# One core, a two-layer decoder trunk in split float32: the split weights stored 136 columns apart instead of 128

## The reference

```
for l in range(2):
    h = rmsnorm(x, norm1)
    z = h @ w_in                       # 1024 -> 6400 columns: attention, convolution, recurrence, gates
    ya, yb, yc = dilated_attention(z), gated_convolution(z), hgrn2_recurrence(z)
    mix = g0 * (ya @ w_pa) + g1 * (yb @ w_pb) + g2 * (yc @ w_pc)
    x = x + mix @ w_o
    h2 = rmsnorm(x, norm2)
    x = x + square(relu(h2 @ w_up)) @ w_down      # 1024 -> 4096 -> 1024
y = rmsnorm(x, norm_f)
```

## Time and profile before

| | |
|---|---|
| runs of the kernel | 811.49, 812.18 and 812.16 us, median 812.16 |
| profiled execution: span from first to last instruction | 809.8 us |
| profiled execution: its own time with what lies around the span | not shown; the median run is 2.4 us over the span |
| TensorE busy with matmuls, with weight loads | 99%, 98% of the span |
| VectorE, ScalarE, GpSimd busy | 70%, 54%, 34% |
| granted TensorE clock, mean of the span | 0.997 of full |
| matmul instructions | 6786 |
| HBM read, written | 191.17 MB, 51.90 MB |

### The profile page before, as it was taken

How to read it: one execution, slowest core, us unless ns; L and a number is a source line. 1 busy time by engine, 2 the same in 40 slices (tenths; PEclk the granted TensorE clock), 3 DMA queues, 4 the chain that set the end, 5 groups by cost and what they waited for, 6 DMA issues and landing times.

```text
span 809.8 us, 17686 instructions
## 1 busy us (share of the span) xinstructions
PE 801.3 (99%) x6786; PEld 789.7 (98%) x6786; DVE 570.3 (70%) x774; ACT 439.6 (54%) x627; POOL 274.7 (34%) x246
## 2 busy tenths in 40 slices
PE   8999999999999999999999999999999999999996
PEld 8999999999999999999999999999999999999996
DVE  6978898577877665545577788966797666645552
ACT  6663667545557664444354637674455666644442
POOL 3599293055700000122149827702663000001220
PEclk9999999999999999999999999999999999999998
DMA  8797779868567688777558968986765767787751
GB/s 327 226 342 279 279 236 328 229 226 314 185 208 226 215 287 285 257 239 250 190 179 225 359 244 289 278 254 232 271 225 178 247 235 250 240 285 241 253 207 53
DMA packets 125721, 199.88 MB, mean 247 GB/s; under 512 B 19680, under 2 KB 115376, under 8 KB 118192
## 3 DMA queue, kind: packets, MB, share of 16 engines
q1 hardware_dynamic: 124368, 196.48, 72.3%
q10 hardware_dynamic: 1296, 2.61, 0.9%
HBM read 191.17 MB, written 51.90 MB: 300 GB/s over the span
## 4 chain that ended last, share of the span: by engine, by line
PE 98%; DVE 1%; DMA 1%; ACT 0%; DVEq 0%; ACTq 0%; issue 0%
PE main L695 29%; PE main L696 28%; PE main L697 28%; PE small L697 1%; PE small L696 1%; PE small L695 1%; PE small L711 1%; PE small L740 1%; PE small L754 1%; DMA raw<-in_w_in 1%; PE main L680 1%; PE main L681 0%; PE main L684 0%; PE small L792 0%; PE main L671 0%; PE small L928 0%
## 5 line engine op out<-in xcount | busy, mean ns | idle before, releaser
L1043 ACT ACTIVATE w_hi<-raw 128x1024 fp32r<-128x1024 f32 (+1 forms) x256 | 266.4, 1043 | 234.3 <-PE main L697 148.6
L1292 DVE TENSOR_TENSOR w_lo<-raw,w_hi 128x1024 fp32r<-128x1024 f32 (+1 forms) x256 | 340.8, 1332 | 65.5 <-ACT w_hi L1043 64.5
L695 PE MATMUL main<-h_hi,w_hi 128*128 128x264 f32 x1248 | 357.9, 287 | 0.0
L696 PE MATMUL main<-h_lo,w_hi 128*128 128x264 f32 x1248 | 354.0, 284 | 0.0
L697 PE MATMUL main<-h_hi,w_lo 128*128 128x264 f32 x1248 | 353.9, 284 | 0.0
L695 PEld LDWEIGHTS main<-h_hi,w_hi 128*128 128x128 f32 x1248 | 235.3, 189 | 3.0 <-DVE w_lo L1292 1.5
L696 PEld LDWEIGHTS main<-h_lo,w_hi 128*128 128x128 f32 x1248 | 235.5, 189 | 0.1
L697 PEld LDWEIGHTS main<-h_hi,w_lo 128*128 128x128 f32 x1248 | 234.2, 188 | 0.0
L695 PE MATMUL main<-a_hi,w_hi 128*128 128x264 f32 x512 | 145.4, 284 | 0.0
L697 PE MATMUL main<-a_hi,w_lo 128*128 128x264 f32 x512 | 145.2, 284 | 0.0
L696 PE MATMUL main<-a_lo,w_hi 128*128 128x264 f32 x512 | 145.2, 284 | 0.0
(11 more groups left out here) (241 smaller groups left out, 1042.5 us busy)
## 6 DMA issues: line engine op xcount, KB each, us to landing
raw<-in_w_in SPq DMA_DIRECT2D x48, 1024.0 KB, 6.3
raw<-in_w_up SPq DMA_DIRECT2D x32, 1024.0 KB, 5.3
raw<-in_w_down SPq DMA_DIRECT2D x32, 1024.0 KB, 5.4
out_kvs<-in_cache SPq DMA_DIRECT2D x48, 512.0 KB
out_kvs<-in_cache SPq DMA_DIRECT2D x32, 496.0 KB
raw<-in_w_o SPq DMA_DIRECT2D x8, 1024.0 KB, 6.0
raw<-in_w_br SPq DMA_DIRECT2D x8, 768.0 KB, 4.8
gates<-q_scratch SPq DMA_DIRECT2D x4, 768.0 KB, 7.9
```

What stands on the lines that cost most here:

```text
L695: pe.matmul(out[:, 0:TOK], wh, rh, start=start and k == 0, stop=False)
L696: pe.matmul(out[:, 0:TOK], wh, rl, start=False, stop=False)
L1043: act.activation(w_hi[:, slot(l, u), 0:k, :], raw_of(u, k), ACT.Copy).then_inc(w_hi_ready, 1)
L1292: dve.tensor_tensor(w_lo[:, slot(l, u), 0:k, :], raw_of(u, k), w_hi[:, slot(l, u), 0:k, :].bitcast(F32), ALU.subtract).then_inc(w_lo_ready, 1)
```

## The change

A k tile of `w_hi` and `w_lo` takes 136 columns instead of 128; the last 8 hold nothing. So the start of a weight row moves on by 544 bytes (2 x 256 + 32) per k tile, and by 32 within 256, as that of a moving row does. Unused tiles of 3 and 7 lines of 32 bytes are put before `gates` and before `mix_hi`. `kv_s`, `v_s` and `q_s` become parts of one tile `sample_heads`, at partitions 0, 32 and 64. No instruction is added, taken away or moved in order.

```diff
 O_IN, O_O, O_UP, O_DN, OUTS = 0, 50, 58, 90, 98
 RING = 4
+LINE = 8
...
         raw = sb("raw", [P, 3, KT, 2 * P])
-        w_hi = sb("w_hi", [P, RING, KT, P], F32R)
-        w_lo = sb("w_lo", [P, RING, KT, P], F32R)
+        w_hi_rows = sb("w_hi_rows", [P, RING, KT, P + LINE], F32R)
+        w_lo_rows = sb("w_lo_rows", [P, RING, KT, P + LINE], F32R)
...
+        sb("before_gates", [P, 3 * LINE])
         with ExitStack() as early:
             gates = sb("gates", [P, N_GATE, TOK], stack=early)
             z = sb("z", [P, CT_GATE, TOK], stack=early)
             kv_tm = sb("kv_tm", [P, 2, NG, 2, P], stack=early)
-            kv_s = sb("kv_s", [SAMPLES, NG, 2, P], stack=early)
-            q_s = sb("q_s", [SAMPLES, NG, P], stack=early)
+            sample_heads = sb("sample_heads", [P, NG * 2 * P], stack=early)
             kg = sb("kg", [P, 2, TOK], stack=early)
             v_tm = sb("v_tm", [P, 2, 2, P], stack=early)
-            v_s = sb("v_s", [SAMPLES, 2, P], stack=early)
...
         with ExitStack() as s:
             sb("gates_below", [P, N_GATE, TOK], stack=s)
+            sb("before_mix", [P, 7 * LINE], stack=s)
             mix_hi = sb("mix_hi", [P, KT, TOK], F32R, stack=s)
...
+        w_hi, w_lo = (t[:, :, :, 0:P] for t in (w_hi_rows, w_lo_rows))
+        kv_s = sample_heads[0:SAMPLES, :].rearrange("p (g k c) -> p g k c", g=NG, k=2)
+        v_s = sample_heads[32:32 + SAMPLES, 0:2 * P].rearrange("p (a c) -> p a c", a=2)
+        q_s = sample_heads[64:64 + SAMPLES, 0:NG * P].rearrange("p (g c) -> p g c", g=NG)
```

## The result

The changed kernel takes 813.24 us (median of 16 runs, 813.06 to 814.01), the one before 811.9 us (median of 16, 811.45 to 812.49). The ratio is 1.0019, with a 95% interval of 1.0012 to 1.0026: slower by 0.2%, where 805.7 us was forecast. It lies 0.2 us above the range.

The account below looks back on a forecast made before the run. TensorE was taken as the bound: number of matmuls times their step. Terms of 5.0, 3.3, 0.4 and 0 us summed to 8.7, taken as 6.5: 803.3 us span, plus 2.4 for the median run, 805.7 us; range 797.5 to 813.0.

Parts of the forecast that it names:

- R: Moving row's start less weight row's start, within 256 bytes; claimed to set each matmul's step, 115.8 to 128.7 ns.
- The list of eight by k: Steps at k = 0 to 7 in `w_up`, the same one place earlier in `w_down`; claimed to stop differing by k.
- Rival 1: Only the moving row's own address counts in the matmuls: mean step stays, 812.2 us, no change; 0.14 together with rival 4.
- rival 4: Matmul histories wash out the differences, leaving the mean over the eight R: no change; 0.14 together with Rival 1.
- The nearest that before has: Matmul steps after the change read off the old positions: 8.7 us less in sum, three quarters taken, 6.5 us.
- C: Step from L697 to the next L695, loading the next k tile's weights; taken for h as 121.7 ns.
- A: Step from L695 to L696 in a k tile; taken for h, at R = 0, as 120.8 ns.
- B: Step from L696 to L697 in a k tile; taken for h, at R = 0, as 116.3 ns.
- Rival 2: In h k tiles C becomes dear: 7 ns x 1312 = 9.2 us more, 814.9 us, slower; chance 0.12.
- Rival 3: Matmul streams settle in a cheap rhythm, all h, a and mix steps at 116.3 ns: 28 us less, 784 us; 0.07.
- The leftover 10 ns: Part of each 120.8 ns matmul step beyond 110 ns of moving columns; likeliest reading: moving reads and weight loads interfere.
- The other edits: Splits writing rows 544 bytes apart, sample rows' copies and stores moved by partitions, small matmuls' operands shifted; splits costed at nothing.

Follow-up runs that it names:

- the best version: Changed kernel with the high parts of h, a, mix and y at R = 64, the low parts at R = 224; 798.14 us, ratio 0.9831 to the kernel before.
- the eight equal pairs on the way up: Changed kernel plus matmul stretches behind its last one, both parts at R = 0, 32, ... 224; steps 121.4, 121.8, 119.7, 120.3, 124.7, 122.5, 121.4, 121.0 ns.

## Why the prediction was wrong

**What bounds the kernel: right.** The steps of the 5952 matmuls explain 1.6 of the 1.7 us, and they explain the 14 us of the best version too. Three readings on the way were off and carry nothing: L695 to L697 have 85% of the chain under `main` and 3 more under `small`, not 86; ScalarE with splits 10% slower would be busy 58% and not 57; and each run lies 1.7 to 1.9 us over its own span (811.57 over 809.8), not 2.4, which set a median against another run's span.

**That R sets the step: right, as far as it went.** As the tiles are declared, all starts lie at the remainders worked out. The list of eight by k vanished (at R = 0 an alternation of two k tiles stands in its place, which was not expected), and places without the stride changed nothing (ratio 0.9997). Rival 1 fell, rival 4 as well, since the steady steps are far apart (118.05 to 124.7); those of the eight equal pairs on the way up have a mean of 121.6, not 120.8. That the time came out near these two rivals' 812.2 is chance: `w_in` and `w_up` lost 2.5 us, `w_down` and `w_o` won 1.0.

**"The nearest that before has": the step that failed.** The sum took C from one k tile and A and B from another, and three quarters of it. For h: 5.0 us less forecast in full, and measured `w_in` 1.7 and `w_up` 0.8 us more. For a: 3.3 less forecast, 0.8 less measured; mix 0.4 and 0.2. A at R = 0 cost 120.8 before and 122.6 in the steady state, C 121.7 before and 122.3 to 124.1, B 116.3 before and 117 and 120 by turns. The runs showed two things in its place. First, a steady relation has a rhythm of its own. Before, a k tile at R = 0 began where a tile at 224 had left off; now it begins where a tile at 0 left off. Second, one relation can have two stable rhythms: at R = 128, 120.3 and 124.7 ns, from identical instructions, and what ran ahead decides which. At R = 0, 121.4 and 122.5 stand side by side in `w_in`. No row of before can show either. The prediction had this as its last sign of being wrong, a dependence on history that the 24 positions don't hold. It named the history and took a quarter off for it, but history isn't a discount on such a sum, it takes away the sum's basis: for h, the sign was wrong.

**Rival 2** had the right place: C did become dearer in h, by 0.6 to 2.4 ns, but not by the 7 it was priced at, and A took part by 1.8. **Rival 3**, a cheap rhythm that locks in, exists (118.05) but not at the pairs that this change chose.

**The leftover 10 ns: read wrongly.** The prediction set 120.8 against 110 and took the likeliest cause of the whole to be the two reads. With 64 weight columns in the kernel it was still 120.3, with 32 in the stretches 120.3, with everything standing still 120.0. Most of it is a price per matmul with its load that no placing tried here removes (8 ns are left in the cheapest pair). So the far end, "every step at 110", was out of reach, and what the best placing found here wins is 3 ns a step and not 11. The 112.5 ns that the prediction set beside the trace has no term for the weight load of each matmul, and was seen in no run at 264 columns.

**The other edits at nothing: right.** The splits have the same times, the waits for `w_lo` are 1.5 us as before, the other matmuls and the sample rows' tile are in the 0.1 us of "all else".

What stays open is why. The runs show that both addresses within 256 bytes count, and that a state carries over from one matmul to the next. That the two reads get in each other's way is still an argument from this: which gives way to which, and why the steps stand at few values, was only seen from outside. Nor was it tried how the rhythm of a kernel would hold over many more launches; the runs of each kernel here agree within 0.2%.

## What to carry to other kernels

Where one engine runs the same instruction thousands of times, average its start-to-start distance by position in the loop: a pattern that goes by address is a cost that can be moved, but a step out of the varied pattern is no price for a steady one. Run the steady pattern by itself behind the kernel, with the neighbours it will have: 64 pairs took one kernel, and 119.7 and 118.05 came back in the real one. But give each place more than one thing to run ahead of it: 128 had 124.7 in that kernel and 120.3 in the changed one. Before the distance to the ideal is taken for the prize, change one size and see what part of it is fixed; here it was 8 of 11 ns.

## What the runs showed of the hardware that was not expected

- The step of a matmul with its own weight load depends on where its moving rows and the weight rows start within 256 bytes, in the kernel before between 115.8 and 128.7 ns by position, for 264 columns at the granted 2.4 GHz. The Trainium skill ("TensorE: Matmul & The Clock Gate", Part 2, step 1) calls the two read ports independent. Here the place of one read relative to the other changes the step, and the measurement decides.
- The same stretch at the same addresses runs at 120.3 or 124.7 ns a step, depending on what ran ahead of it, and keeps to it for at least 192 matmuls; in the kernel with h moved, `w_down` keeps the dear one throughout, and `w_in` has both.
- Most steady steps stand at few values: 54 of 64 pairs at 120.3, 121.4, 121.8, 122.5, 123.6 or 124.7 ns; the lowest seen are 118.05 and 119.7.
- Beside its columns, a matmul with its own load costs 8 to 15 ns at 264 columns, and 11 to 12.5 at R = 0 (118.1 at 256 columns, 112.1 at 240), down to a floor of 111.6 from 224 columns on.
